# Mixture of experts: a fourth way through an expert pair, for up to 64 tokens per expert, on one Trainium2 core

## What is computed

```
def hier_moe(x, rg_w, rg_b, re_w, re_b, w_gu, w_down):
    g_p, g_idx = top_k(softmax(t @ rg_w + rg_b), 1)          # one of 4 groups
    e_p, e_idx = top_k(softmax(e_logits of that group), 2)   # two of its 8 experts
    gate, expert = (g_p * e_p / sum(e_p)), g_idx * 8 + e_idx
    for every expert e, on the tokens that chose it:
        hg, hu = split(xb @ w_gu[e], 2)                      # 1024 -> 2 x 512
        y = (silu(hg) * hu) @ w_down[e]                      # 512 -> 1024
    out[token] += gate * y
```

## Time and profile before

| | |
|---|---|
| median of 3 runs | 2189.8 us (2189.2 to 2190.83) |
| the profiled execution, its own time | 2188.98 us |
| its span in the profile | 2187.1 us |
| PE busy, share of the span | 1798.6 us, 82% |
| DMA in the two mixtures | near 425 GB/s, elsewhere 77 to 207 GB/s |
| chain that ended last | PE 69%, DMA 18%, issue 5%, DVE 5%, ACT 3% |

### The profile page before, as it was taken

The page is one execution under the profiler, slowest core; times in us unless marked ns, Lnnn a source line. Parts: engine busy times, 40 slices in busy tenths (PEclk is TensorE's granted clock), DMA queues, the critical chain, the costliest instruction groups (busy, mean ns, idle before and its releaser), DMA issues.

```text
span 2187.1 us, 30973 instructions
## 1 busy us (share of the span) xinstructions
PE 1798.6 (82%) x13574; PEld 1128.6 (52%) x13574; DVE 598.5 (27%) x1032; ACT 393.8 (18%) x760; POOL 36.0 (2%) x28
## 2 busy tenths in 40 slices
PE   6999999999999987766666878799987777876664
PEld 4788884879886764322222332575984332322211
DVE  1132312123421145221111211564345221211102
ACT  2333211313301143100000100241222010100001
POOL 0000000000000000000000000001030000000000
PEclk9999999999999998888788899899998798988977
DMA  9322333333243533899999997213004899999995
GB/s 340 97 89 97 135 137 145 141 77 135 77 154 139 207 116 150 370 425 425 425 426 425 425 400 291 77 58 117 4 23 177 365 424 426 422 425 425 425 425 224
DMA packets 51465, 539.53 MB, mean 247 GB/s; under 512 B 7440, under 2 KB 16272, under 8 KB 18224
## 3 DMA queue, kind: packets, MB, share of 16 engines
q1 hardware_dynamic: 49248, 527.06, 59.2%
q0 software_dynamic: 1152, 6.29, 0.8%
q10 hardware_dynamic: 848, 3.00, 0.4%
HBM read 535.28 MB, written 1.05 MB: 245 GB/s over the span
## 4 chain that ended last, share of the span: by engine, by line
PE 69%; DMA 18%; issue 5%; DVE 5%; ACT 3%; DVEq 0%; ACTq 0%
PE ps L410 53%; PE ps L417 13%; DMA arena<-in_moe_w_gu 6%; DMA ring<-in_moe_w_gu 5%; DMA arena<-in_moe_w_down 3%; DMA ring<-in_moe_w_down 3%; PE ps L423 3%; DVE x L1369 1%; ACT arena L2171 1%; DVE arena L1358 1%; ACT hb L2167 1%; DVE mT L1945 1%; DVE mT L1948 0%; ACT arena L2442 0%; ACT arena L2167 0%
## 5 line engine op out<-in xcount | busy, mean ns | idle before, releaser
L410 PE MATMUL ps<-hT,ring 128*128 128x256 f32 (+2 forms) x1888 | 391.1, 372 | 0.0
L410 PEld LDWEIGHTS ps<-hT,ring 128*128 128x128 f32 (+2 forms) x1888 | 330.7, 185 | 52.7 <-issue 3.4
L417 PE MATMUL ps<-arena 128*32 128x512 f32 (+1 forms) x1572 | 240.8, 698 | 102.6 <-issue 67.1
L417 PE MATMUL ps<-ring,arena 128*32 128x512 f32 x1472 | 213.1, 713 | 106.0 <-issue 72.5
L2171 ACT ACTIVATE arena<-ps 128x512 f32<-128x512 f32 (+4 forms) x145 | 94.5, 652 | 895.8 <-PE ps L417 519.3
L410 PE MATMUL ps<-arena 64*64 64x64 f32 (+10 forms) x1944 | 186.5, 322 | 56.3 <-ACT arena L2442 22.2
L1358 DVE TENSOR_TENSOR arena<-arena,ps 128x256 f32<-128x256 f32 (+2 forms) x82 | 46.0, 561 | 551.2 <-ACT arena L2167 464.2
L417 PEld LDWEIGHTS ps<-arena 128*32 128x32 f32 (+1 forms) x1572 | 64.5, 130 | 256.2 <-issue 202.0
L410 PEld LDWEIGHTS ps<-arena 64*64 64x64 f32 (+4 forms) x1944 | 113.8, 159 | 130.8 <-ACT arena L2442 53.4
L417 PEld LDWEIGHTS ps<-ring,arena 128*32 128x32 f32 x1472 | 53.3, 126 | 245.7 <-issue 194.4
L410 PE MATMUL ps<-ring,hT 128*128 128x256 f32 (+4 forms) x576 | 149.4, 418 | 8.7 <-ACT hT L2167 6.9
(11 more groups left out here) (173 smaller groups left out, 1259.2 us busy)
## 6 DMA issues: line engine op xcount, KB each, us to landing
ring<-in_moe_w_gu SPq DMA_DIRECT2D x64, 2048.0 KB, 28.7
arena<-in_moe_w_gu SPq DMA_DIRECT2D x64, 2048.0 KB, 31.2
arena<-in_moe_w_down SPq DMA_DIRECT2D x32, 2048.0 KB, 33.4
ring<-in_moe_w_down SPq DMA_DIRECT2D x32, 2048.0 KB, 33.4
ring<-in_w_merge SPq DMA_DIRECT2D x16, 2048.0 KB, 7.6
ring<-in_w_in SPq DMA_DIRECT2D x10, 2048.0 KB, 7.5
ring<-in_attn_w_qkv SPq DMA_DIRECT2D x6, 2048.0 KB, 7.3
ring<-in_rw_w_rkv SPq DMA_DIRECT2D x6, 2048.0 KB, 7.7
```

The lines of the kernel that those rows point to most:

```text
L410: i = t.matmul(o, l, r, start=first, stop=last, skip_group_check=True)
L417: i = t.matmul(o, l, r, start=first, stop=last, skip_group_check=True)
```

## The change

The m way becomes a function `several(pr, before, R)` on PE, DVE and ACT, with R rounds. A third flag, `e.flag3` (more than 64), is written by DVE beside the other two and read inside the m branch: R = 3 (called m3) if set, else R = 2 (m2). Both bodies are written out for each of the 32 pairs, m3 first and m2 behind it. In m2 the third round of each chunk is gone, the later tokens are gathered with 64 columns instead of 128, and the third block of transposes, sigmoid, products and eviction is gone, as are the two pairs of back matmuls of r = 2.

```diff
-    e.flag, e.flag2 = (carve(16).bitcast(mybir.dt.int32) for _ in range(2))
+    e.flag, e.flag2, e.flag3 = (carve(16).bitcast(mybir.dt.int32) for _ in range(3))
...
+            ts(cnt2, cnt, 2 * CAP + 0.5, None, ALU.is_gt, None)
+            cp(e.flag3, cnt2)
...
+        def several(pr, before, R):
...
+            w2 = 2 * CAP * (R - 1)
             for half in range(2):
-                        mm([(psum[1][:, k * P:(k + 1) * P], x[:, i, k * P:(k + 1) * P], e.oh2[:, i * P:(i + 1) * P], i == 0, i == 1)
+                mm([(psum[1][:, k * P:k * P + w2], x[:, i, k * P:(k + 1) * P], e.oh2[:, i * P:i * P + w2], i == 0, i == 1)
...
-                            mm_to([o for r in range(1 if q < 2 else 0, 3) for o in gu_round(r, q)], before + 8 + q, N + f"gu{q}")
+                    mm_to([o for r in range(1 if q < 2 else 0, R) for o in gu_round(r, q)], before + 8 + q, N + f"gu{q}")
...
-                        for r in range(3):
+                for r in range(R):
                     if q == 0:
                         t.wait_ge(*dve(N + W + f"hs{r}"))
...
+                    more = t.value_load(e.flag3[0:1, pr:pr + 1], min_val=0, max_val=1)
+                    with t.If(more != 0):
+                        several(pr, before, 3)
+                    with t.Else():
+                        several(pr, before, 2)
```

More of the change, by code:

```diff
@@ L948, in moe @@
                 with t.Else():
[L950 to L967, removed]
@@ L970, in moe @@
[L970 to L981, removed]
@@ L1001, in moe @@
[L1001 to L1030, removed]
@@ L1904, in moe @@
                 with v.Else():
[L1905 to L1919, removed]
[L1920 to L1934 removed]
+                    more = v.value_load(e.flag3[0:1, pr:pr + 1], min_val=0, max_val=1)
+                    with v.If(more != 0):
+                        several(pr, before, 3)
+                    with v.Else():
+                        several(pr, before, 2)
             with v.Else():
@@ L2442, in last, with several, later @@
             s.activation(o, a, ACT.Copy).then_inc(*act.to(count, name))
+        def several(pr, before, R):
+            N, N1, W = M + f"{pr} ", M + f"{pr + 1} ", f"m{R} "
+            act.n = before
+            def later(a):
+                return a.rearrange("p (k c) -> p k c", k=KT)[:, :, 0:2 * CAP * (R - 1)]
+            s.wait_ge(*pe(N + W + "tokens0"))
+            cp(later(e.x2)[:, 0:4], later(psum[1])[:, 0:4], N + W + "x")
+            s.wait_ge(*pe(N + W + "placesT"))
+            cp(e.ogT2[0], pt[:, 0:256])
+            if R > 2:
+                cp(e.ogT2[1], pt[:, 256:512])
+            s.wait_ge(*pe(N + W + "gu0"))
+            cp(e.gu, pg[:, 0:512], N + W + "gu0 out")
+            if R > 2:
+                s.wait_ge(*pe(N + "gu3"))
+                cp(e.gu2[1], psum[0][:, 0:512], N + W + "gu2 out")
+            src = (psum[0][:, 512:1024], psum[1][:, 0:512], psum[1][:, 512:1024])
+            for r, sg in enumerate((e.sg, *e.sg2)[:R]):
+                g5 = src[r].rearrange("p (k a c n) -> p k a c n", k=4, a=2, c=2)
+                s.wait_ge(*pe(N + W + f"guT{r}"))
+                fn(sg, g5[:, :, :, 0], ACT.Sigmoid, N + W + f"sig{r}")
+            next_four(pr, pt, N + W)
+            s.wait_ge(*pe(N + W + "dn0"))
+            if R > 2:
+                cp(e.yb, pg[:, 0:512], N + W + "yb0")
+                s.wait_ge(*pe(N + "dn1"))
+                last(e.yb2[1], psum[0][:, 0:512], before + 15, N1 + "all in")
+            else:
+                last(e.yb, pg[:, 0:512], before + 15, N1 + "all in")
         s.wait_ge(*pe(M + "first gather0"))
@@ L2465, in moe @@
                 with s.Else():
[L2466 to L2485 removed]
+                    more = s.value_load(e.flag3[0:1, pr:pr + 1], min_val=0, max_val=1)
+                    with s.If(more != 0):
+                        several(pr, before, 3)
+                    with s.Else():
+                        several(pr, before, 2)
             with s.Else():
```

164 lines of the change are left out of this document (112 added, 52 removed).

## The result

The changed kernel takes **2207.85 us** (median of 4 runs, 2205.23 to 2210.58), the kernel before in the same rounds 2189.5: ratio **1.0084, 95% interval 1.0071 to 1.0097**, slower by 18.4 us. The forecast was 2194.1 us, with a range up to 2199.5. Of the two directions the chances had favoured slower (0.43 against 0.11), with 0.46 on no change that can be told; the time lies 13.8 us above the forecast and outside the range. The profiled execution took 2206.48 us (before: 2188.98), with a span of 2204.7 us.

The account below looks back on a forecast made before the run. PE was taken to bound pairs 12 and 14 of the first mixture, transfers the second mixture. 0.8 + 7.7 + 5.9 + 0.8 - 10.9 = +4.3 us gave 2194.1 us on the median; range 2186 to 2199.5.

Parts of the forecast that it names:

- What m2 saves, 10.9 us: Pair 14 of the first mixture: six rounds 10.3, two transposes 0.26 and the shorter wait before down 0.3 us saved.
- Third flag 0.8: On PE's way into m pairs: one more flag load and its untaken branch cost pair 12 0.8 us.
- entry into m2 7.7: Ahead of pair 14, first mixture: third branch jumps over m3, 7.0 us, plus 0.7 for the flag load.
- exit of m3 5.9: End of pair 12, first mixture: the exit jumps over m2 and s, 6.2 us instead of 0.31, so 5.9 more.
- Two more DVE operations, 0.8: Start of each mixture: making the third flag shifts the transfers by 0.4 us, 0.8 us in all.
- The cost of a jump ends with the jump: PE's branches: the branch's duration was taken as its price, long jumps 6.2 to 7.05 us, a short one 0.31.
- Rival 3: Pair 14's exit from m2 over s becomes long through moved code: 5.9 us more, 2200.0 us; chance 0.08.
- Nothing in pair 5 of the second mixture can show, transfers never pause: Second mixture: transfers set its end, so pair 5's 7.7 us entry and 10.9 us saving both stay hidden.
- Rivals 1, 2 and 4: m3's exit short (0.15), 2188.2 us; both new jumps short (0.10), 2181.3; pair 14 takes m3 (0.02), 2204.
- rival 2: Entry into m2 and exit of m3 both short jumps: 8.5 us faster, 2181.3 us; chance 0.10.

Follow-up runs that it names:

- experiment 1: The changed kernel with each pair's m body chosen at build time, no third flag, third branch or second body: 2174.85 us, ratio 0.9942 to the kernel before.
- experiment 4: Never-executed dead matmuls in both kernels lay every s target 200 to 203 instructions ahead of its block's end: changed kernel 2189.83 us (0.9999), kernel before 2188.81 (1.0).
- Experiment 6: The changed kernel with dead matmuls laying targets well in the first mixture only, the second's block positions as in the changed kernel: 2194.49 us, ratio 1.0026.
- experiment 5: The kernel before with dead matmuls laying every s target only 12 to 15 instructions ahead of its block's end: 2260.43 us, ratio 1.0333.
- experiment 9: One m body, PE skipping only the third round's matmuls in eight short jumps, targets laid well by dead matmuls: 2180.89 us, ratio 0.9964 to the kernel before.
- experiment 8: The kernel before with ways not taken left out on PE and replaced by dead matmuls, giving jumps of 25 to 521 instructions: 2163.4 us, ratio 0.989.

## Why the prediction was wrong

Point by point, by its own steps.

- **What m2 saves, 10.9 us: right.** 10.5 in experiment 1, and 10.0 with the two branches in experiment 4. The gather of 64 columns takes 3.79 us, of 128 columns 3.84, both at full clock: no gain, as taken.
- **Third flag 0.8, entry into m2 7.7, exit of m3 5.9: right**, at 0.6 to 0.9, 7.2 to 7.4 and 5.5 to 6.1 us.
- **Two more DVE operations, 0.8: not seen**, and too small to be told.
- **The cost of a jump ends with the jump: wrong, and this is the step that failed.** The prediction took a branch record's duration, and PE's idle time up to the landing, for the whole price. Behind a landing there is a second wait, which I take to be for the block after the target's, and its size hangs on where the target stands: 4.30 us in pair 15, and 6.6 us for that pair with the low clock around it, against the same pair laid well. Rival 3 named the dependence on block starts, but laid it on one branch, m2's exit, priced it at 5.9 us and gave it 0.08. It lay elsewhere: it can come in the first rounds of any pair, in this kernel in pair 15's. The trace of before had it, as 0.92 us of "issue" in pair 12 that I passed over as small; a wait on nothing, in the middle of a run of equal matmuls, needs a reason whatever its size. Laid well, the change gives 2189.83, which is 1.0 above the kernel before laid as well; the forecast's terms say 4.3. Pair 15's 2.2, which is the clock again, and the flag's 0.8 make most of the rest, both too small for these intervals.
- **"Nothing in pair 5 of the second mixture can show, transfers never pause": wrong.** Its entry costs 7.7 us as forecast (1856.1 to 1863.8), and its shorter body does save (laid well, 38.9 us from start to start for 51.6), but the stall of 3.66 us at its start, low clock behind it (its first 32 records end 11.2 us after they begin, at a mean granted clock of 0.57, for 3.4 at full clock) and 2.16 us at its exit together empty the slack: behind the issue of transfers at 1896.88 the next comes only at 1915.95, and the transfers run low for some 5 us from 1912. Laid well the pause is gone (experiment 4). Experiment 6 puts the second mixture's part at 4.7 us by the medians; its profiled execution, though, takes 456.1 us for that mixture and that of experiment 4 takes 454.3, 1.8 less.
- **Rivals 1, 2 and 4 fell**: the exit was long (6264 ns), the entry too (6485 ns), and m2 was taken in pair 14. The Trainium skill, Advanced Engine Details and Errata, section Control Flow Timing, gives a compare-and-branch about 108 ns, by which rival 2 would have come true. The row of 6485 ns is nowhere near it; the measurement decides.

**What stays open.** That the second wait is a fetch of the next block is inferred from where the stalls begin and from how they moved, grew and went with dead code alone; no view shows the fetch itself. Why it comes some 6 us after the landing, rather than along with the target's block, and in the six short cases of experiment 5 after 3, is not known. Experiment 6 starts its second mixture 14.4 us earlier than the changed kernel (1714.52 for 1728.96): 2.6 are an earlier first round and 0.3 the stretch to pair 11, 7.1 are pairs 12 to 15 (6.8 of them pair 15: the stall and the low clock behind it), and 4.3 are the RWKV layer. The first of these is of a size by which kernels differ anyway (887.6 to 890.2), and the last has no branches: it takes 347.7 us in the changed kernel and 343.4 here, but 346.0 in the kernel before, 343.2 in experiment 1 and 348.4 with dead code in the kernel before. Between the changed kernel and experiment 6 most of it is the granted clock. From 100 to 160 us behind the end of pair 15, in the changed kernel and then in experiment 6:

```profile
1481.25:1541.25 60.00, 57.45 (x583) 33.26 (x584) 30.41 (x27) 13.60 (x12) 7.98 (x4) 0.89 0.36 136
```

```profile
1471.14:1531.14 60.00, 57.19 (x808) 33.47 (x802) 32.52 (x29) 15.70 (x14) 7.97 (x4) 0.97 0.38 142
```

The clock is 0.89 in the one and 0.97 in the other; over the whole layer PE is busy 3.6 us longer and idle 0.7 longer. With the dead code in the kernel before it is 0.86 there; the 2.8 us between the kernel before and experiment 1, both at 0.97, are open. What lowers the clock in some programs I did not find, and no run singled it out. So of the 18 us that came with the placement, some 4 in the profiled executions are a clock in a layer without branches, and their tie to it is not shown.

## What to carry to other kernels

Where PE's program has long branches, its time depends on where their targets fall in blocks of the program, and an edit anywhere ahead of them changes all of these places: here 18 us for a change that costs 1 by itself, and 71 at the worst placement tried. Before you believe a difference of a per cent between two such kernels, move both by some dead code, or lay their targets alike, and compare again. And leave out work with short jumps around single groups of instructions rather than with a second body. Here the jump over the first body cost some 7 us and the one over the second some 6, while the eight short jumps of experiment 9 left a few tenths.

## What the hardware showed that I had not expected

- A jump on PE costs 0.2 to 0.44 us into the same block of 256 instructions or the next one, 377 instructions included, and 5.9 to 6.9 us two blocks on, 345 included (experiment 8; three jumps into the next block took 0.84 to 5.4 us).
- After a long jump to a target 2 to 7 matmul records ahead of its block's end PE stalls a second time, most often 3.3 to 4.9 us, until some 6 us after the landing.
- Dead code of 128 instructions, never executed, made one kernel some 11 us faster and another 14.6 us slower.
- Where the jump into an s pair was short (experiment 8), the idle time ahead of the pair fell from 5 to 0.3 us; with these and the shorter jumps into the m pairs the whole took 27 us less.
- The same 32 matmul records of pair 15 took 3.64 us at a granted clock of 1.00 and 5.28 at 0.68; a layer without branches differed by 4 us between programs, most of it by the clock.
